# One decoder layer with routed experts on one core: earlier weight loads, a third buffer for down weights, one store per block, gathers in pairs

## What is computed

```
x  = LN(alpha*x + (1+gate1)*mix)
h2 = x*(1+scale2) + shift2
x  = LN(alpha*x + (1+gate2)*MoE(h2))

def moe(h, w_router, router_bias, w_e_gate, w_e_up, w_e_down):
    ...                                   # every token gets 2 of 16 experts, with weights
    for e in range(N_EXPERTS):
        he = jax.nn.silu(h @ w_e_gate[e]) * (h @ w_e_up[e])
        y = y + gate[..., e:e + 1] * (he @ w_e_down[e])
```

## Time and profile before

| | us |
|---|---|
| median of 3 runs | 1132.91 |
| lowest and highest | 1125.71, 1134.81 |
| the profiled execution | 1129.62 |
| its span in the trace | 1127.8 |
| PE busy in the span | 1004.3 (89%) |

### The profile page before, as it was taken

One profiled execution on the slowest core, in us unless ns is written; L12 is line 12 of the kernel. 1 busy time (PEld: TensorE's weight loads), 2 busy tenths in 40 slices (PEclk: granted clock), 3 DMA queues, 4 the chain that ended last, 5 costly groups with the idle time before them and its releaser, 6 DMA issues. The chain is left out here.

```text
span 1127.8 us, 22134 instructions
## 1 busy us (share of the span) xinstructions
PE 1004.3 (89%) x8978; PEld 673.7 (60%) x8978; DVE 490.9 (44%) x1259; ACT 186.9 (17%) x451; POOL 231.3 (21%) x260
## 2 busy tenths in 40 slices
PE   4699999998899998999999999976999999998930
PEld 3477777544776666677777764564655555554510
DVE  0211799982447788865114004676133011110118
ACT  2200012112222211221111110111111111111102
POOL 1300012635221122313325440001000000000044
PEclk9799999999998998999999999986999999999965
DMA  9932643647604305114072317133879999999864
GB/s 310 339 62 77 198 151 112 227 152 283 225 24 140 76 28 166 49 43 118 10 184 60 112 45 301 66 117 160 320 288 358 383 419 367 387 391 398 323 154 122
DMA packets 93572, 218.43 MB, mean 194 GB/s; under 512 B 23696, under 2 KB 42503, under 8 KB 89373
## 3 DMA queue, kind: packets, MB, share of 16 engines
q1 hardware_dynamic: 71428, 183.83, 45.3%
q0 software_dynamic: 5936, 19.16, 5.2%
q10 hardware_dynamic: 16113, 14.06, 4.2%
HBM read 198.95 MB, written 21.06 MB: 195 GB/s over the span
## 5 line engine op out<-in xcount | busy, mean ns | idle before, releaser
L1642 PE MATMUL bank<-arena 128*128 128x288 f32 (+5 forms) x2034 | 510.3, 408 | 8.7 <-issue 4.2
L1642 PEld LDWEIGHTS bank<-arena 128*128 128x128 f32 (+1 forms) x2034 | 371.3, 193 | 138.7 <-issue 49.4
L2005 PE MATMUL bank<-arena 128*32 128x256 f32 x3136 | 181.8, 383 | 11.4 <-issue 7.6
L2005 PEld LDWEIGHTS bank<-arena 128*32 128x32 f32 x3136 | 103.8, 109 | 81.2 <-issue 15.0
L1593 DVE TENSOR_TENSOR arena<-arena,bank 128x128 f32<-128x128 f32 x49 | 14.2, 290 | 235.9 <-ACT arena L1063 235.8
L2024 PE MATMUL bank<-arena 128*32 128x256 f32 x1568 | 94.6, 381 | 0.0
L801 POOL TENSOR_SCALAR arena<-arena 128x288 f32<-128x288 f32 x48 | 46.2, 963 | 218.6 <-ACT arena L1025 218.6
L1137 DVE SCALAR_TENSOR_TENSOR arena<-arena 128x512 f32<-128x512 f32 x120 | 82.0, 746 | 0.0
L1646 PE MATMUL bank<-arena 128*128 128x128 f32 (+6 forms) x327 | 51.2, 294 | 33.3 <-DMA arena<-in_x_sample 9.2
L1646 PEld LDWEIGHTS bank<-arena 128*128 128x128 f32 (+6 forms) x327 | 39.2, 156 | 47.8 <-issue 18.7
L2024 PEld LDWEIGHTS bank<-arena 128*32 128x32 f32 x1568 | 45.9, 108 | 31.9 <-issue 2.0
(11 more groups left out here) (266 smaller groups left out, 835.3 us busy)
## 6 DMA issues: line engine op xcount, KB each, us to landing
arena<-in_w_e_gate SPq DMA_DIRECT2D x16, 2048.0 KB, 11.4
arena<-in_w_e_up SPq DMA_DIRECT2D x16, 2048.0 KB, 16.1
arena<-in_w_e_down SPq DMA_DIRECT2D x16, 2048.0 KB, 10.8
arena<-in_w_ada SPq DMA_DIRECT2D x12, 2048.0 KB, 12.3
arena<-in_w_in SPq DMA_DIRECT2D x10, 2048.0 KB, 10.5
expert_rows<-arena POOLq DMA_DIRECT2D x1, 5120.0 KB, 18.5
arena<-in_x_prompt SPq DMA_DIRECT2D x8, 512.0 KB, 5.4
expert_rows<-arena ACTq DMA_DIRECT2D x28, 96.0 KB, 7.4
```

The source lines that it names most:

```text
L1642: last = pe.matmul(out, a, b, start=k == 0, stop=k == len(pairs_) - 1)
L2005: last = pe.matmul(out, HG[:, g % 2, k, a:a + BLK], gate_up[i % 2][:, :, k, c * P:c * P + P], start=k == 0, stop=k == KT - 1)
```

## The change

Seven edits, all around the experts.

1. SP issues gate and up of turn 1 as soon as PE has released the `wo` weights, ahead of the last h2 store, and down of turn 1 behind that store.
2. The second h2 instruction is cut into two halves of 512 columns; the first half of the transposes waits for the first half alone.
3. Down weights get three slots of their own (`down_ring`, the third over the arrays XR and R, which are free by then) and semaphores of their own. Down of turn i is issued when turns 0 to i-3 have had their `down`, for turn 2 when `weights_up` has come.
4. BC2 moves to another place in memory and is loaded at turn 9, not 5.
5. The stores: one DMA for each block, with all 128 partitions as source and a DRAM pattern of [4, 32, 256], after a wait for ACT's own result. 49 stores take the place of 64; `STORED[i]` counts them.
6. The waits on stores use those counts.
7. POOL's gathers at the end are issued as first 0, 1, 2, second 0, first 3, second 1, first 4, second 2, 3, 4. The wait for the last turn's stores stands ahead of second 0.

```
+A_DOWN3 = A_XR
-A_BC2 = A_XR
+A_BC2 = A_HG + 2 * D
...
+    STORED = [16 * sum(NB_AT[i % 2:i + 1:2]) for i in range(NE)]
...
+    down_ring = [ring[2], ring[5], V(A_DOWN3, SLOT)]
+    def expert_down(sp, e, z):
+        w = I["w_e_down"][0]
+        w = w[e] if type(e) is int else w[bass.ds(e, 1)].rearrange("e k n -> (e k) n")
+        sp.dma_start(down_ring[z].rearrange("p (k n) -> p k n", k=NJ), w.rearrange("(k p) n -> p k n", p=P)).then_inc(ev(f"down_in{z}"), 16)
...
             if t >= 1:
-                sp.wait_ge(ev("h2_ready"), t)
+                sp.wait_ge(ev("h2_ready"), 2 * t)
                 sp.dma_start(h2_d[(t - 1) * P:t * P, :], H2[:, (t - 1) % 2, :]).then_inc(ev(f"h2_out{(t - 1) % 2}"), 16)
-        sp.wait_ge(ev("h2_ready"), NT)
+        sp.wait_ge(slot_out, rel[("wo", 1)])
+        expert_weights(sp, 1, 3)
+        expert_weights(sp, 1, 4)
+        sp.wait_ge(ev("h2_ready"), 2 * NT)
         sp.dma_start(h2_d[SEQ:NTOK, :], H2[0:NS, 0, :]).then_inc(ev("h2_out0"), 16)
-        sp.wait_ge(slot_out, rel[("wo", 1)])
-        for z in range(3):
-            expert_weights(sp, 1, 3 + z)
+        expert_down(sp, 1, 1)
...
-            if i == 5:
+            if i == 9:
...
             expert_weights(sp, e, z)
             expert_weights(sp, e, z + 1)
-            sp.wait_ge(ev("dn_full"), FIRST[i - 1])
-            expert_weights(sp, e, z + 2)
+            if i >= 3:
+                sp.wait_ge(ev("dn_full"), FIRST[i - 2])
+            else:
+                sp.wait_ge(ev("weights_up"), 1)
+            expert_down(sp, e, i % 3)
...
-        for t in range(NT):
+        def first_rows(t):
...
-        pool.wait_ge(ev("yo_out1"), 64 * (NE // 2))
-        for t in range(NT):
+        def second_rows(t):
             n = rows_of(t)
+            if t == 0:
+                pool.wait_ge(ev("yo_out1"), STORED[15])
             pool.wait_ge(ev(f"first_in{t}"), 16)
...
+        for t in range(NT + 2):
+            if t < NT:
+                first_rows(t)
+            if t >= 2:
+                second_rows(t - 2)
...
-                    act.wait_ge(ev(f"yo_out{i % 2}"), 64 * (i // 2))
+                    act.wait_ge(ev(f"yo_out{i % 2}"), STORED[i - 2])
...
-                if d in ends:
-                    act.wait_ge(ev("yo_up"), d + 1)
-                    rows = y_d[FIRST[i] * BLK:FIRST[i + 1] * BLK, :].rearrange("(b t) f -> t b f", t=BLK)
-                    for c in range(4):
-                        act.dma_start(rows[:, :, 256 * c:256 * c + 256], YR[BLK * c:BLK * c + BLK, i % 2, 0:NB_AT[i], :]).then_inc(ev(f"yo_out{i % 2}"), 16)
+                y = YR[:, i % 2, d - FIRST[i], :]
+                act.activation(y, banks[6 + d % 2][:, 0:256], ACT.Copy, scale=WBLK[:, d:d + 1]).then_inc(ev("yo_up"), 1)
+                act.wait_ge(ev("yo_up"), d + 1)
+                act.dma_start(bass.AP(y_d.tensor, d * BLK * D, [[256, 4], [D, BLK], [1, 256]]), y).then_inc(ev(f"yo_out{i % 2}"), 16)
...
-                    stt(h2, h2, rs, BC["sh" + pick][0:n], ALU.mult, ALU.add).then_inc(ev("h2_ready"), 1)
+                    for z in range(2):
+                        c2 = slice(512 * z, 512 * z + 512)
+                        stt(h2[:, c2], h2[:, c2], rs, BC["sh" + pick][0:n, c2], ALU.mult, ALU.add).then_inc(ev("h2_ready"), 1)
...
-                pe.wait_ge(ev("h2_ready"), t + 1)
+                pe.wait_ge(ev("h2_ready"), 2 * t + h + 1)
...
-                pe.wait_ge(ev(f"w_in{3 * (i % 2) + 2}"), 16 * (i // 2 + 1))
+                pe.wait_ge(ev(f"down_in{i % 3}"), 16 * (i // 3 + 1))
```

More of the change, by code:

```diff
@@ L139 @@
 A_HG = A_G + 2 * D
-A_HE = A_HG + 2 * D
+A_DOWN3 = A_XR
+A_HE = A_XR
 A_HET = A_HE + 2 * DE
 A_Y = A_HET + 2 * DE
+assert A_Y + 2 * D <= A_DOWN3 + SLOT
 A_YR = A_MG
@@ L149 @@
 A_GA = A_RING2
-A_BC2 = A_XR
+A_BC2 = A_HG + 2 * D
+assert A_BC2 + 4 * D <= A_X1
 A_O = A_H2
@@ L456, in build_in @@
     turn_of = [i for i in range(NE) for _ in range(NB_AT[i])]
-    ends = {FIRST[i + 1] - 1: i for i in range(NE)}
+    STORED = [16 * sum(NB_AT[i % 2:i + 1:2]) for i in range(NE)]
     tile_behind = {max(4 * g - 2, 3): g for g in range(1, TILES)}
@@ L592, in build_in @@
     sp_order.sort(key=lambda x: x[0])
+    down_ring = [ring[2], ring[5], V(A_DOWN3, SLOT)]
[3 more added lines that the diff above has]
+        sp.dma_start(down_ring[z].rearrange("p (k n) -> p k n", k=NJ), w.rearrange("(k p) n -> p k n", p=P)).then_inc(ev(f"down_in{z}"), 16)
     def expert_weights(sp, e, z):
-        name, k = [("w_e_gate", KT), ("w_e_up", KT), ("w_e_down", NJ)][z % 3]
+        name, k = [("w_e_gate", KT), ("w_e_up", KT)][z % 3]
         w = I[name][0]
         w = w[e] if type(e) is int else w[bass.ds(e, 1)].rearrange("e k n -> (e k) n")
-        rows = "(k p) n -> p k n" if z % 3 == 2 else "(p k) n -> p k n"
-        sp.dma_start(ring[z].rearrange("p (k n) -> p k n", k=k), w.rearrange(rows, p=P)).then_inc(ev(f"w_in{z}"), 16)
+        sp.dma_start(ring[z].rearrange("p (k n) -> p k n", k=k), w.rearrange("(p k) n -> p k n", p=P)).then_inc(ev(f"w_in{z}"), 16)
     @block.sync
@@ L673, in _ @@
             if t == 1:
-                for z in range(3):
-                    expert_weights(sp, 0, z)
+                expert_weights(sp, 0, 0)
+                expert_weights(sp, 0, 1)
+                expert_down(sp, 0, 0)
             if t >= 1:
-                sp.wait_ge(ev("h2_ready"), t)
+                sp.wait_ge(ev("h2_ready"), 2 * t)
                 sp.dma_start(h2_d[(t - 1) * P:t * P, :], H2[:, (t - 1) % 2, :]).then_inc(ev(f"h2_out{(t - 1) % 2}"), 16)
-        sp.wait_ge(ev("h2_ready"), NT)
+        sp.wait_ge(slot_out, rel[("wo", 1)])
+        expert_weights(sp, 1, 3)
+        expert_weights(sp, 1, 4)
+        sp.wait_ge(ev("h2_ready"), 2 * NT)
         sp.dma_start(h2_d[SEQ:NTOK, :], H2[0:NS, 0, :]).then_inc(ev("h2_out0"), 16)
-        sp.wait_ge(slot_out, rel[("wo", 1)])
-        for z in range(3):
-            expert_weights(sp, 1, 3 + z)
+        expert_down(sp, 1, 1)
         sp.wait_ge(ev("order_known"), 1)
@@ L709, in further_weights @@
             sp.wait_ge(ev("dn_full"), s + (NBLK - 1))
-            expert_weights(sp, e, 3 * p + 2)
+            expert_down(sp, e, 1 - p)
         each_further(sp, nov, further_weights)
@@ L847, in _ @@
                 pool.indirect_dma_start(G[:, z, :], None, h2_d, bass.IndirectOffsetOnAxis(ints[:, c:c + 1], 0)).then_inc(ev(f"rows_gathered{z}"), 16)
-        pool.wait_ge(ev("yo_out0"), 64 * (NE // 2))
-        pool.wait_ge(ev("yo_out1"), 64 * (NE // 2 - 1))
+        pool.wait_ge(ev("yo_out0"), STORED[14])
+        pool.wait_ge(ev("yo_out1"), STORED[13])
         with pool.If(nov > 0):
-            pool.wait_ge(ev("yo_out1"), 64 * (NE // 2))
+            pool.wait_ge(ev("yo_out1"), STORED[15])
         for s in range(NOV):
             with pool.If(nov > s):
-                pool.wait_ge(ev(f"yo_out{s % 2}"), 64 * (NE // 2) + 16 * (s // 2 + 1))
-        for t in range(NT):
+                pool.wait_ge(ev(f"yo_out{s % 2}"), STORED[14 + s % 2] + 16 * (s // 2 + 1))
+        def first_rows(t):
             n = rows_of(t)
@@ L1088, in further @@
             act.wait_ge(ev("dn_full"), s + (NBLK + 1))
-            act.wait_ge(ev(f"yo_out{p}"), 16 * i + 64 * (NE // 2))
+            act.wait_ge(ev(f"yo_out{p}"), 16 * i + STORED[14 + p])
             w = WSL[:, bass.ds(s + TILES, 1)]
@@ L2020, in down @@
                 pe.wait_ge(ev("yo_up"), b - 1)
-            w = ring[3 * (i % 2) + 2].rearrange("p (k n) -> p k n", k=NJ)
+            w = down_ring[i % 3].rearrange("p (k n) -> p k n", k=NJ)
             for k in range(NJ):
@@ L2066, in further @@
             pe.wait_ge(ev("yo_up"), s + NBLK)
-            pe.wait_ge(ev(f"w_in{3 * p + 2}"), 16 * i + 16 * (NE // 2 + 1))
-            w = ring[3 * p + 2].rearrange("p (k n) -> p k n", k=NJ)
+            pe.wait_ge(ev(f"down_in{1 - p}"), 16 * i + 16 * (len(range(1 - p, NE, 3)) + 1))
+            w = down_ring[1 - p].rearrange("p (k n) -> p k n", k=NJ)
             group(banks[6], [(HET[:, p, k, :], w[:, k, 0:512]) for k in range(NJ)])
```

3 lines of the change are left out of this document (1 added, 2 removed).

## The result

The changed kernel takes 1146.57 us (median of 4 runs, 1141.67 to 1147.60), the kernel before 1130.11 us in the same runs: 1.0139 times as long, 95% interval 1.0102 to 1.0175. It is slower, as forecast, but by 16 us and not 37. Rival (b), 1139 to 1147, had the number.

A forecast was written before the change was run, and what follows sets the result against it. PE and the DMA engines were both taken as near their limits in the experts' stretch; 1129.6 + 40 (four engines) + 3 (clock) - 3 (first gather) - 3 (tail) gave 1166.6, so 1167 us, range 1138 to 1190.

The forecast's parts named there:

- Rival (b): Experts' stores: four engines, but much extra work overlaps with weights, 15 to 23 us remain; 1139 to 1147 us; chance 10%.
- What bounds the kernel: Experts' stretch, 845 to 1070 us: PE and DMA both near their limits, DMA share 0.96, PE busy 214.83 of 225 us.
- Four engines: Block stores with 4 outermost in DRAM should run on four engines, each with 32 rows of 1 KB per block.
- The price: Experts' stretch: stores on four engines add 43.9 us of work to each, lengthening it by 34 to 44; 40 us taken.
- How it reaches PE: Stores pile up; ACT's waits for stores of turn i-2, 10 us and more each, delay Silus, products and PE; issuing free.
- Clock: Long gaps in the experts' stretch cost PE its clock, two to four times 1.69 us; 3 us taken, bounds 0 and 8.
- Third buffer and BC2: Experts' weights: earlier down could give back at most 9.9 us, BC2 between 0 and 4.4; 0 taken for both.
- rival (a): Experts' stores use all sixteen engines, gaps give back 0 to 9.9 us; 1114 to 1124 us, faster; chance 13%.
- First gather: Before the first expert block: early weights of turn 1 take 0.7 to 3.4 us off PE's 8.43 us wait; 3 taken.
- Tail: After PE's end: fewer store issues and reordered gathers save between 1 and 6 us; 3 us taken.

The follow-up runs named there:

- e1: Changed kernel with each block's store written as one run of [128, 256] in DRAM, output rows in another order; 1120.20 us, 0.9935 of the kernel before.
- e2: Changed kernel with four stores a block, each of 32 partitions with outermost dimension 32; 1124.67 us, 0.9963 of the kernel before.
- e3: Changed kernel with the four stores per turn of the kernel before, all else as changed; 1121.09 us, 0.9931 of the kernel before.
- e4: Kernel before with only the change's one store per block and the counts that belong to it; 1148.04 us, 1.0171 of the kernel before.
- e5: Changed kernel with two stores a block, 64 partitions each, DRAM pattern [2, 32, 256]; 1216.76 us, 1.0766 of the kernel before.
- e10: Changed kernel with the old stores per turn and down weights issued late as before the change; 1129.33 us, 0.9984 of the kernel before.
- e8: Kernel before with only the last gathers issued in pairs; 1131.89 us, 1.0011 of the kernel before.
- e9: Changed kernel with each block's store one run in DRAM written as [8, 16, 256]; 1122.74 us, 0.9921 of the kernel before.
- e13: Changed kernel with block stores as [8, 16, 256], neighbouring rows of a group apart in DRAM; 1128.28 us, 0.9998 of the kernel before.
- e6: Changed kernel storing only the first 64 of every 256 numbers, plus one early DMA of zeros; 1144.79 us.

## Why the prediction was right or wrong

**What bounds the kernel.** Right: the experts' stretch is where a load on the DMA engines shows, where it is 20.0 us longer; the other stretches together give 2.0 back.

**Four engines.** Right, and shown: the share of a lone store (two tenths), its 4 completion packets, and e1, e2, e3 and e4, which move the whole loss with the number of engines. Before the result it was an estimate carried over from the shares of 51.0% and 49.8% with 8 outermost; these are means over the engines, and no row names the ones that worked.

**The price.** This is where it failed. I took 40 us for the four engines; the whole stretch, clock included, grew by 20.0. The step that failed is the addition: "These four then need 225 x (0.956 + 0.195) = 259 us of work", and so 34 us more at the least. The DMA view of the changed kernel from 845 to 1090 us (245 us, the same part of the work and 20 us longer) has:

```profile
q1 hardware_dynamic: 10188, 75.57, 76.6%
q10 hardware_dynamic: 4884, 4.85, 5.7%
q0 software_dynamic: 1152, 4.19, 4.4%
```

- The work itself was nearly right. The 6.5% of q10 are 4864 rows and 768 completion packets in 234 us, the 5.7% here 4736 rows and 148 completions in 223 us. From the two a row takes 0.047 us and a completion 0.008 us (the trace's packet records: 0.0467 and 0.009). So 38 blocks of 24 more rows add 42.6 us, where I had 43.9 from a mean of both kinds.
- On the four engines q10's share is four times 5.7%, 22.8%. With 81.8% from q1, q0 and instruction fetch (0.8%) that makes 104.6%: 256 us of packets in 245 us. So packets overlapped on an engine for 11 us at least, and a share of 0.956 was no proof that only 4.4% was left. (The trace does not name a packet's engine. That a weight DMA uses all sixteen, its completions show: before, from 750 to 775 us, three of them, the last h2 store and the first gather leave 80, 16 each. That the weights are spread evenly is the prediction's own premise. By it e4 has 103.5% on its four engines from 845 to 1090 us, e5 102.4% on its two from 845 to 1160.)
- "If they idle as much as now ... by 44 us. I take 40 us" left 6 us of idle time unused. By these shares none was left.

So the 40 us come down to 20: 6 us of idle time that was used, 3 us of work less (256 and not 259), 11 us of overlap. The overlap is a remainder and not timed by itself; if the four engines idled at all, it was larger. What makes packets overlap no run shows. This is the engines' account of the whole 20 us; that of PE, 13.4 us idle and 6.6 us of slower clock, is the same 20 us seen from the other side.

Rival (b), which had the number, had its reason in part too: it let 4 to 12 of its 37 us overlap and used all 9.9 us of idle time. It was given 10%.

**How it reaches PE.** The wait for the stores of turn i-2 came as said, 28.0 us in four waits, though "more than 30" was forecast; landings of 27 to 31 us were longer than my 10 to 25. The gaps in the middle of turns came too, the longest of 7.2 us and not 10, and the DMA share fell to 0.87 and not towards 0.80. Wrong was "Issuing costs ACT nothing: one DMA of 0.33 to 0.75 us per block": single issues took up to 11.55 us. The bound of 25 us that I gave for the lost cover assumed a constant issue time. That the weights' landing sets the pace was wrong for four engines: up weights landed 15.5 us after their issue (median from 845 us on), where it was 16.9. The pace was set by the stores, through ACT.

**Clock.** I took 3 us, with bounds of 0 and 8; it is 6.6, a third of the loss. Before, one stretch ran at half clock after a gap, behind 1027.68: the granted clock was 1.00 up to there, so it had not dropped while PE idled, and 0.50 from 1028.00 to 1031.20. After, there are four, at 0.50 to 0.53: near 948 to 958, 1013 to 1016, 1044 to 1047 and 1075 to 1078 us, with gaps of PE of 7.24, 3.37, 2.47 and 1.95 us that ended at 952.43, 1011.63, 1043.33 and 1073.88. After the 7.24 us gap the 32 matmuls of a `down` take 3.64 us and not 1.93:

```profile
952.80 3.64 PE L2050 MATMUL bank<-arena 128*32 128x256 f32 x32
```

**Third buffer and BC2.** Nought in the end with four engines, as said: e4, which has neither, has the same stretch to 0.1 us. The changed kernel did gain the 2.60 us gap at turn 6, and lost it again behind the stores. 2.5 us with spread stores (e10), less than the 9.9 I allowed in rival (a): the gap at turn 13 stays at 4 us in e1 to e3.

**First gather.** Right: 3.3 us, in the trace 4.37 us from issue to landing instead of 7.7.

**Tail.** 3 forecast, 1.3 measured. DVE's first tile came 13.95 us after PE's end, before 17.54, so 3.6 us were won, more than forecast. "Later tiles take DVE 5.1 us each, the gathers 3.1, so nothing else is late" was wrong, as e8 shows: the second tile and POOL's power gave 2 us back.

**Rival (a)** has its own answer: on sixteen engines the same change gives 1120 us (e1), inside its 1114 to 1124.

## What to carry to other kernels

Read the outermost dimension on both sides of a DMA before merging several into one: four stores with 32 outermost became one with 4 (16 completions a store, then 4), the bytes stayed, and the experts' stretch grew by 20 us; e3, the changed kernel with its old stores, is the best version here that keeps all results, 0.9931 of the kernel before. When work is moved onto a few engines of a shared pool, price it per engine and subtract the whole idle time that those engines have in the stretch; what was left here was larger than one minus the DMA share, since packets overlapped (11 us by the sum above), and beyond it, from four to two engines, nearly the full price was paid (0.0445 us a row, where one alone takes 0.047). Price PE's clock with the gaps: here it was a third of the loss (6.6 of 20.0 us). The queue that fell behind stalled not only those who waited for its data but also ACT, which issues (11.55 us for a store that takes 0.58 us otherwise), so count an issue as "free" only while its queue drains.

## What the runs showed of the hardware that was not expected

- Issuing a store from ACT took 0.58 us in 34 of 49 cases and up to 11.55 us while three stores took 27 to 31 us to land on four engines (21.39 us for the two of a block on two engines), and ACT ran nothing else in that time.
- In these runs the issue time went with the form of the pattern, not with the number of engines: 0.35 us for one run of 128 rows, 0.57 to 0.63 us for three dimensions on 16, 4 and 8 engines.
- A pattern of [8, 16, 256] whose dimensions join without a gap behaved as one of 128 rows (e9), on sixteen engines by its 16 completion packets a store; the same shape with rows apart used half of them (e13, 8 completions).
- A store row of 1 KB took an engine 0.047 us, one of 256 bytes 0.018 us (e6), a completion packet 0.009 us.
- The shares of the queues on the engines in use added up to more than one: 1.046 on four engines in the changed kernel, 1.024 on two in e5, if the weights are spread evenly.
